# Token group outside, three passes inside: reordering the matmuls of a feature tile

## The chip, the cores and the metric

The kernel runs on one core of one Trainium2 chip. The metric is the device time of one execution in microseconds (us); lower is better.

## What is computed

One layer of a hybrid decoder trunk, for a prompt of 1024 tokens and 8 samples of 8 tokens (1088 tokens in all, model width 1024, fp32 throughout), which share all weights:

```
h = rmsnorm(x, norm_ffn1) * (1 + sc1) + sh1
x = x + 0.5 * g1 * (silu(h @ w1_gate) * (h @ w1_up)) @ w1_down
u = rmsnorm(x, norm_mix) * (1 + sc2) + sh2
p = u @ w_in + b_in       # conv value, conv gate, q, k, v, o, gate_a, gate_b, i, f
A = conv module of the conv columns  (GLU, causal depthwise conv 31, layer norm, silu, @ w_conv_out)
B = mLSTM of q, k, v, i, f in chunks of 128, head norm, sigmoid(o) *, @ w_mlstm_out
x = x + g2 * ((sigmoid(gate_a) * A + sigmoid(gate_b) * B) @ w_out)
h = rmsnorm(x, norm_ffn2) * (1 + sc3) + sh3
x = x + 0.5 * g3 * (silu(h @ w2_gate) * (h @ w2_up)) @ w2_down
y = rmsnorm(x, final_norm)
```

The shifts, scales and gates come from `silu(c) @ w_ada + b_ada`. The new convolution and mLSTM states are outputs too.

## The kernel before

Activations lie with features on the 128 partitions and tokens along the free dimension, as 8 feature tiles (`KT`) of 1092 columns. The tokens are cut in three groups, `GROUPS`, of 364, 364 and 360 columns.

**Weight units.** All large products use weight units of 128 x 1024 values, 220 of them in a fixed order. SyncE loads a unit into `w_raw` (two buffers). GpSimd splits it: `w_hi` is the value rounded to fp32r (line 543), `w_lo` the rest (line 545). It overwrites the halves of a buffer only after TensorE has reported that unit as done (`unit_done`). Activations are split in the same way, `u_hi` and `u_lo` (`hid_hi` and `hid_lo` in the feed-forward blocks, `a_hi` and `a_lo` for the convolution output).

**The three passes.** A product with fp32 quality is the sum of three fp32r products: hi weights with hi activations, hi weights with lo activations, lo weights with hi activations. `three_passes` (line 570) issues them for one feature tile `k`: pass outside, token group inside, nine matmuls. Each group accumulates in a PSUM bank of its own: `slots[:, s, g, ...]`, where a slot `s` of two has three banks.

**Who calls it.** `project` (line 579) handles a unit that is 8 feature tiles of one output tile: 8 x 9 = 72 matmuls. `project_pair` (line 594) does two units at once, alternating between them per tile. `down` (line 611) uses a unit for four output tiles with two feature tiles each, again 72 matmuls. The one unit that runs beside the gate rows (lines 693 to 702) calls it as well; the nine matmuls of line 697, with weights of 36 columns, are written out there and keep their own order.

**What stands around it.** TensorE waits, ahead of the nine matmuls, for the split weights (`w_split`), a free slot (`slot_free`) and where needed for the tile's activations (`ready`). The only increment is on the last matmul of a unit or part. The readers, VectorE and ScalarE, then take all three banks of the slot in one instruction (`bank3`).

**The heads.** The middle of the kernel runs over 4 heads. In `section_a` TensorE does 8 units while VectorE computes the 31 convolution taps of two tiles (`taps`, recorded as line 1072). In `section_b` the units are interleaved with small fp32 matmuls of the mLSTM, the pieces (lines 740 to 775), which write `bank_x` and `bank_y`. Half of a tile's pieces are issued after its nine matmuls (`between`), the other half inside `three_passes` (`middle`), ahead of the third pass. The first piece of a head waits for VectorE's taps and what follows them (line 748 in the waits).

TensorE records one LDWEIGHTS row and one MATMUL row for each fp32r matmul; an fp32 matmul appears as two of each.

Of the kernel before, what the change touches and what calls it, by code (L numbers as in the profile page):

```python
# [37 lines left out]
GROUPS = [(0, GW), (GW, 2 * GW), (2 * GW, NT)]  # L38
# [89 lines left out]
def trunk(nc, t_in, t_out):  # L128
    with ExitStack() as ctx:
# [12 lines left out]
        def own(name, shape, dt=F32):  # L142
            return place(name, shape, dt, region(int(np.prod(shape[1:])) * 4))
# [3 lines left out]
        w_hi = own("w_hi", [P, 2, D], F32R)  # L147
        w_lo = own("w_lo", [P, 2, D], F32R)
# [408 lines left out]
        def _(pe):  # L557
# [10 lines left out]
                return s  # L568

            def three_passes(s, w_of, hi, lo, k, K, middle=None):  # L570
                for q, (w, r) in enumerate(((w_hi, hi), (w_hi, lo), (w_lo, hi))):
                    if middle and q == 2:
                        middle(k)
                    for g, (a, b) in enumerate(GROUPS):
                        last = pe.matmul(slots[:, s, g, 0:b - a], w_of(w), r[:, k, a:b],  # L575
                                         start=(k == 0 and q == 0), stop=(k == K - 1 and q == 2))
                return last

            def project(hi, lo, ready=None, base=0, between=None, middle=None):

                s = open_slot()
                u = jobs.unit.n % 2
                pe.wait_ge(w_split, jobs.unit(1))
                for k in range(KT):
                    if ready is not None:
                        pe.wait_ge(ready, base + k + 1)
                    last = three_passes(s, lambda w: w[:, u, k * P:(k + 1) * P], hi, lo, k, KT, middle)
                    if k == KT - 1:
                        last.then_inc(unit_done, 1)
                    if between:  # L590
                        between(k)
                jobs.take_unit()

            def project_pair(hi, lo, ready, base=0, between=None):

                s, u = open_slot(), jobs.unit.n % 2
                pe.wait_ge(slot_free[1 - s], jobs.used(1))
                pe.wait_ge(w_split, jobs.unit(2))
                for k in range(KT):
                    pe.wait_ge(ready, base + k + 1)  # L600
                    for n in range(2):
                        v = (u + n) % 2
                        last = three_passes((s + n) % 2, lambda w: w[:, v, k * P:(k + 1) * P], hi, lo, k, KT)
                        if k == KT - 1:
                            last.then_inc(unit_done, 1)
                    if between:
                        between(k)
                jobs.take_unit()
                jobs.take_unit()

            def down():

                pe.wait_ge(hid_ready, hid())
                for half in range(2):
                    u = jobs.unit.n % 2
                    pe.wait_ge(w_split, jobs.unit(1))
                    for m in range(4):
                        s = open_slot()
                        for k in range(2):
                            last = three_passes(s, lambda w: w[:, u, k * 512 + m * P:k * 512 + (m + 1) * P],  # L620
                                                hid_hi, hid_lo, k, 2)
                        if m < 3:
                            last.then_inc(part_done, 1)
                            jobs.take_part()
                        else:
                            last.then_inc(unit_done, 1)
                            jobs.take_unit()
# [84 lines left out]
            for n in range(4):  # L712
# [3 lines left out]
                for j in range(4):  # L716
# [3 lines left out]
                    else:  # L720
                        a = NP + (4 * (n - 2) + j) * TB
# [946 lines left out]
```

## Time and profile before

| | us |
|---|---|
| median of 3 runs | 3418.8 |
| lowest and highest | 3417.13, 3423.22 |
| span of the profiled execution | 3417.0 |
| PE busy in it | 3167.0 |
| DVE busy | 1597.9 |
| GpSimd (POOL) busy | 1020.0 |
| ScalarE (ACT) busy | 465.6 |

The times are those of whole executions, the profile is of one of its own. PE is the matmul part of TensorE and PEld its weight loads. Rows of matmuls overlap: what one matmul costs in a stream is the distance from start to start. In a timeline a row merges instructions of a kind, named after the first; its us run from the first start to the last end.

### The profile page before, as it was taken

What the parts mean: (1) busy time and instruction counts of PE and PEld (TensorE: products, weight loads), DVE (VectorE), ACT (ScalarE), POOL (GpSimd) and SP (SyncE); (2) the same over time, 40 slices, a digit from 0 to 9 for tenths busy, and PEclk for the clock granted to TensorE, in tenths of its full rate; (3) what the DMA queues carried; (4) which work ended last, traced back from release to release, by engine and by line L of the source; (5) the groups of instructions that cost most, each with busy time, mean ns of one, the idle gap of its engine ahead of it and who ended that gap; (6) DMA issues with size and microseconds to landing.
All of it is one profiled execution on the core that took longest, in us unless ns stands there. A gap on an engine that the chain in (4) does not pass through costs nothing.

```text
span 3417.0 us, 47244 instructions
## 1 busy us (share of the span) xinstructions
PE 3167.0 (93%) x18860; PEld 3029.7 (89%) x18860; DVE 1597.9 (47%) x2811; ACT 465.6 (14%) x746; POOL 1020.0 (30%) x449
## 2 busy tenths in 40 slices
PE   8999999999968889879888997989998999999995
PEld 8999999999958778878787895789887999999995
DVE  5122233222276943973694397476344233232335
ACT  2000000000031122012112211322012000000001
POOL 1233333333312311321231142034332333333331
PEclk9999999999989999999999998999998999999997
DMA  6312121212121112212211221222210111111111
GB/s 221 106 62 74 61 74 61 74 61 68 49 75 41 44 42 68 70 34 60 74 50 42 68 70 51 60 103 93 108 50 25 44 44 44 47 43 43 43 43 59
DMA packets 83136, 217.63 MB, mean 64 GB/s; under 512 B 28352, under 2 KB 28480, under 8 KB 82496
## 3 DMA queue, kind: packets, MB, share of 16 engines
q1 hardware_dynamic: 83000, 215.86, 19.7%
q8 instruction: 88, 1.44, 0.2%
q14 instruction: 40, 0.33, 0.0%
q10 hardware_dynamic: 8, 0.00, 0.0%
HBM read 184.03 MB, written 31.81 MB: 63 GB/s over the span
## 4 chain that ended last, share of the span: by engine, by line
PE 73%; DVE 16%; issue 5%; DVEq 3%; POOL 1%; DMA 1%; ACT 1%; SPq 0%; ACTq 0%; POOLq 0%
PE slots L575 61%; DVE y L1072 12%; PE bank_x L637 3%; PE bank_x L758 2%; DVEq L1376 2%; PE bank_x L750 1%; PE bank_x L765 1%; PE bank_y L762 1%; PE bank_y L767 1%; DVE work L1100 1%; PE bank_y L637 1%; DMA w_raw<-w_units_dram 1%; PE bank_y L740 1%; PE bank_x L775 0%; PE bank_x L748 0%
## 5 line engine op out<-in xcount | busy, mean ns | idle before, releaser
L543 POOL TENSOR_TENSOR w_hi<-w_raw,one 128x1024 fp32r<-128x1024 f32 x220 | 437.9, 1990 | 2317.9 <-PE slots L575 2247.3
L575 PE MATMUL slots<-u_hi,w_hi 128*128 128x364 f32 (+1 forms) x4032 | 930.3, 339 | 53.0 <-DVE u_lo L1133 20.2
L575 PE MATMUL slots<-u_hi,w_lo 128*128 128x364 f32 (+1 forms) x4032 | 899.5, 332 | 0.0
L575 PE MATMUL slots<-u_lo,w_hi 128*128 128x364 f32 (+1 forms) x4032 | 898.4, 331 | 0.0
L575 PEld LDWEIGHTS slots<-u_hi,w_hi 128*128 128x128 f32 x4032 | 699.4, 191 | 81.4 <-issue 65.4
L575 PEld LDWEIGHTS slots<-u_hi,w_lo 128*128 128x128 f32 x4032 | 705.3, 190 | 9.2 <-issue 8.7
L575 PEld LDWEIGHTS slots<-u_lo,w_hi 128*128 128x128 f32 x4032 | 708.2, 191 | 0.0
L545 POOL TENSOR_TENSOR w_lo<-w_raw,w_hi 128x1024 fp32r<-128x1024 f32 x220 | 581.3, 2642 | 17.2
L1163 DVE TENSOR_TENSOR work<-work,slots 128x1092 f32<-128x1092 f32 x44 | 56.9, 1292 | 913.5 <-PE slots L575 913.5
L1072 DVE SCALAR_TENSOR_TENSOR y<-glu,dw_cur,y 128x1024 f32 (+1 forms) x240 | 344.7, 1436 | 9.1
L1072 DVE SCALAR_TENSOR_TENSOR x<-slots,m_g,x 128x728 f32<-128x728 f32 x368 | 257.8, 742 | 0.0
L575 PE MATMUL slots<-hid_hi,w_hi 128*128 128x364 f32 (+1 forms) x1056 | 237.4, 333 | 11.1 <-DVE hid_lo L1168 9.6
L575 PE MATMUL slots<-hid_lo,w_hi 128*128 128x364 f32 (+1 forms) x1056 | 233.8, 330 | 0.0
L575 PE MATMUL slots<-hid_hi,w_lo 128*128 128x364 f32 (+1 forms) x1056 | 232.3, 328 | 0.0
L575 PEld LDWEIGHTS slots<-hid_hi,w_hi 128*128 128x128 f32 x1056 | 183.6, 190 | 12.1 <-DVE hid_lo L1168 10.0
L885 ACT ACTIVATE hid_hi<-work 128x1092 fp32r<-128x1092 f32 x44 | 49.2, 1118 | 1030.5 <-PE slots L575 733.7
L575 PEld LDWEIGHTS slots<-hid_lo,w_hi 128*128 128x128 f32 x1056 | 183.5, 189 | 0.0
L575 PEld LDWEIGHTS slots<-hid_hi,w_lo 128*128 128x128 f32 x1056 | 183.3, 189 | 0.0
L1146 DVE TENSOR_TENSOR xs_tmp<-slots,m_g 128x64 f32<-128x64 f32 x184 | 41.4, 225 | 289.1 <-PE slots L575 288.1
L1072 DVE SCALAR_TENSOR_TENSOR y<-glus,dw_cur,y 128x64 f32 (+1 forms) x240 | 149.3, 622 | 0.0
L637 PEld LDWEIGHTS bank_x<-cs,ada 128*128 128x128 f32 x896 | 119.4, 212 | 5.3 <-issue 5.3
L637 PE MATMUL bank_x<-cs,ada 128*128 128x9 f32 x896 | 116.2, 267 | 5.3 <-DMA ada<-ada_units_dram 5.3
(219 smaller groups left out, 2187.4 us busy)
## 6 DMA issues: line engine op xcount, KB each, us to landing
w_raw<-w_units_dram SPq DMA_DIRECT2D x220, 512.0 KB, 3.6
ada<-ada_units_dram SPq DMA_DIRECT2D x72, 512.0 KB, 4.2
st<-state_dram SPq DMA_DIRECT2D x32, 257.0 KB, 3.7
C_s_out<-st SPq DMA_DIRECT2D x32, 257.0 KB, 3.6
x_keep<-x SPq DMA_DIRECT2D x1, 4368.0 KB, 12.7
ga_keep<-th SPq DMA_DIRECT2D x8, 546.0 KB, 5.6
gb_keep<-th SPq DMA_DIRECT2D x8, 546.0 KB, 5.6
th<-gb_keep SPq DMA_DIRECT2D x8, 546.0 KB, 4.6
```

The lines of the kernel that those rows point to most:

```text
L543: pool.tensor_tensor(w_hi[:, slot, :], w_raw[:, slot, :], one[:].to_broadcast([P, D]), ALU.mult).then_inc(w_hi_done, 1)
L545: pool.tensor_tensor(w_lo[:, slot, :], w_raw[:, slot, :], w_hi[:, slot, :].bitcast(F32), ALU.subtract).then_inc(w_split, 1)
L575: last = pe.matmul(slots[:, s, g, 0:b - a], w_of(w), r[:, k, a:b], start=(k == 0 and q == 0), stop=(k == K - 1 and q == 2))
L637: last = pe.matmul(b[:, 16 * j:16 * j + NV], ada[:, j, k * P:(k + 1) * P], cs[:, k, :], start=(k == 0), stop=(k == KT - 1))
L740: pe.matmul(bank_y[0:L, 0:L], k_of(m, a, L), q_of(m, a, L), start=(m == 0), stop=(m == 1))
L750: last = pe.matmul(bank_x[0:L, n * P:(n + 1) * P], src, ident[:], start=True, stop=True)
L758: last = pe.matmul(bank_x[0:L, 0:C1], q_of(m, a, L), mem[:, m, :], start=(m == 0), stop=(m == 1))
L885: act.activation(hid_hi[:, j, :], prod, ACT.Copy).then_inc(hid_hi_done, 1)
L1072: return dve.scalar_tensor_tensor(out=out, in0=in0, scalar=scalar, in1=in1, op0=op0, op1=op1)
L1146: dve.tensor_tensor(sample3(xs_tmp[:]), sample3(slots[:, s, 2, LP:LP + NB * TB]), per_batch(g[:, 1:NV]), ALU.mult)
L1163: dve.tensor_tensor(tile3(prod), tile3(sg), bank3(s), ALU.mult).then_inc(slot_free[s], 1)
L1376: dve.drain()
```

## The change

The two loops in `three_passes` change places: the token group becomes the outer loop and the pass the inner one. The call of `middle`, before ahead of the third pass, is now ahead of the third group. The `start` and `stop` flags keep their conditions.

```diff
             def three_passes(s, w_of, hi, lo, k, K, middle=None):
-                for q, (w, r) in enumerate(((w_hi, hi), (w_hi, lo), (w_lo, hi))):
-                    if middle and q == 2:
+                for g, (a, b) in enumerate(GROUPS):
+                    if middle and g == 2:
                         middle(k)
-                    for g, (a, b) in enumerate(GROUPS):
+                    for q, (w, r) in enumerate(((w_hi, hi), (w_hi, lo), (w_lo, hi))):
                         last = pe.matmul(slots[:, s, g, 0:b - a], w_of(w), r[:, k, a:b],
                                          start=(k == 0 and q == 0), stop=(k == K - 1 and q == 2))
                 return last
```

## Rows read from the trace of the kernel before

**Rows 1.** The page: busy time of TensorE, and granted clock in 40 slices.
```profile
PE 3167.0 (93%) x18860; PEld 3029.7 (89%) x18860; DVE 1597.9 (47%) x2811; ACT 465.6 (14%) x746; POOL 1020.0 (30%) x449
...
PEclk9999999999989999999999998999998999999997
```

**Rows 2.** The page: the chain that ended last, share by engine.
```profile
PE 73%; DVE 16%; issue 5%; DVEq 3%; POOL 1%; DMA 1%; ACT 1%; SPq 0%; ACTq 0%; POOLq 0%
```

**Rows 3.** Groups by line: count, busy us, mean ns, idle before.
```profile
L575 PE MATMUL slots<-u_hi,w_hi 128*128 128x364 f32 (+1 forms) x4032 | 930.3, 339 | 53.0 <-DVE u_lo L1133 20.2
L575 PE MATMUL slots<-u_hi,w_lo 128*128 128x364 f32 (+1 forms) x4032 | 899.5, 332 | 0.0
L575 PE MATMUL slots<-u_lo,w_hi 128*128 128x364 f32 (+1 forms) x4032 | 898.4, 331 | 0.0
L575 PEld LDWEIGHTS slots<-u_hi,w_hi 128*128 128x128 f32 x4032 | 699.4, 191 | 81.4 <-issue 65.4
```

**Rows 4.** The chain in order of time: start us, us, what.
```profile
175.23 36.02 PE slots L575 x216
...
2819.89 160.14 PE slots L575 x964
```

**Rows 5.** Timeline of PE from 2999.9 us: start us, us, what.
```profile
2999.97 0.66 PE L575 MATMUL slots<-u_hi,w_hi 128*128 128x364 f32 x3
3000.47 0.67 PE L575 MATMUL slots<-u_lo,w_hi 128*128 128x364 f32 x3
3000.98 0.65 PE L575 MATMUL slots<-u_hi,w_lo 128*128 128x364 f32 x3
3001.47 0.66 PE L575 MATMUL slots<-u_hi,w_hi 128*128 128x364 f32 x3
3001.96 0.66 PE L575 MATMUL slots<-u_lo,w_hi 128*128 128x364 f32 x3
```

**Rows 6.** Busy time by stretch, with the granted clock after the engines.
```profile
150.00:956.00 806.00, 802.02 (x5032) 801.92 (x5031) 227.00 (x393) 47.33 (x43) 270.31 (x122) 1.00 0.19 65
2640.00:3230.00 590.00, 590.00 (x3554) 590.00 (x3553) 171.76 (x288) 36.34 (x33) 218.74 (x98) 1.00 0.14 44
```

**Rows 7.** The waits: us in total, times, longest us.
```profile
DVE work L1163 <- PE slots L575: 913.5, 44, 37.1
```

**Rows 8.** Timeline of the weight loads in the stretch of rows 5.
```profile
3000.31 0.52 PEld L575 LDWEIGHTS slots<-u_lo,w_hi 128*128 128x128 f32 x3
3000.81 0.52 PEld L575 LDWEIGHTS slots<-u_hi,w_lo 128*128 128x128 f32 x3
```

**Rows 9.** Pieces in the timeline; durations min/median/max of lines 758 and 740.
```profile
1253.85 0.59 PE L765 MATMUL bank_x<-vws,ktok 128*128 128x257 f32 x2
1254.28 0.60 PE L767 MATMUL bank_y<-vws,ktok 128*128 128x257 f32 x2
...
1256.30 0.25 PE L740 MATMUL bank_y<-qkvo 128*8 128x8 f32 x4
...
1261.90 1.03 PE L758 MATMUL bank_x<-st,qkvo 128*8 128x257 f32 x4 [0.29 <-DVE b_cur L1072]
...
L758 PE MATMUL bank_x<-st,qkvo x128: 377/380/635, 1220.6 to 2232.6; 128*8 128x257 f32 x128
...
L740 PE MATMUL bank_y<-qkvo x256: 169/224/426, 1178.0 to 2228.3; 128*128 128x128 f32 x64, 128*8 128x8 f32 x64
```

**Rows 10.** The waits of PE: the first piece of a head.
```profile
PE bank_x L748 <- DVE ap_h L1465: 80.9, 4, 25.5
```

**Rows 11.** The chain in order of time: single tiles of nine matmuls.
```profile
1550.90 1.48 PE slots L575 x9
1553.25 1.50 PE slots L575 x9
```

**Rows 12.** Timeline of PE: nine matmuls with 36-column weights, and the next.
```profile
1005.55 0.65 PE L697 MATMUL slots<-u_hi,wg_hi 128*36 128x364 f32 x3
...
1007.00 0.66 PE L575 MATMUL slots<-u_hi,w_hi 128*128 128x364 f32 x3
```

## The prediction

> **What bounds the kernel now.** I read the page's engine lines first: TensorE (PE) is busy 3167.0 of 3417.0 us, and the granted clock stands at 9 in nearly every slice [rows 1]. A busy PE is not yet a bound, so the chain of work that ended last came next: 73% of it is PE and 16% VectorE (DVE) [rows 2]. The groups by line then say which PE work it is: the three kinds of matmul of line 575 come to 4032 each with `u`, and each kind's weight loads are as many as its matmuls [rows 3]. That last point matters here: every matmul loads its own weights, even where the same weights were loaded just before.
>
> Next I looked for the true price of one matmul. The durations in the groups (331 to 339 ns) overlap and are no price; the step from one start to the next is. In the chain, 216 matmuls take 36.02 us and 964 take 160.14 us without a piece of anything else between them [rows 4], so 0.1668 and 0.1661 us each. I take 0.166 us. The timeline of one such stretch shows the same step by step: three matmuls of a pass every 0.49 to 0.51 us [rows 5]. The granted clock there is 1.00, the level of 2.4 GHz [rows 6]. A mean of 362.7 columns (364, 364, 360) at one column a cycle would be 151.1 ns, so 15 ns a matmul are something else. What they are decides the rivals.
>
> **The change part by part.** `three_passes` is called for all 220 weight units. Each has 8 groups of 9 matmuls: 72, in all 15,840, as against 3 x (4032 + 1056 + 192) in the trace. The change permutes the nine inside each group. Nothing is added or removed: the same nine products, the same nine weight loads, the same columns read. Times of one execution: 3417.0 us is the span of the profiled one, 1.8 us under the median of the runs shown, so the sum is made on 3417.0 and 1.8 is added.
>
> Term 1, the waits. Every wait of PE stands ahead of the first of the nine and asks for both halves of the activations, and every increment is on the last of the nine of a unit. DVE reads all three banks of a slot at once and waits for that last one; it waits 913.5 us in total for it at line 1163 [rows 7]. The last matmul stays the ninth, so no reader starts sooner or later. GpSimd, which waits for the same increment, is not moved either. The mLSTM pieces called by `middle` ran after the sixth matmul and still do (before: between pass 2 and pass 3; after: between group 2 and group 3). No DMA is issued from this code and no queue is passed. Cost 0.
>
> Term 2, the weights. The old order changes the stationary data twice per group of nine (to `w_lo`, and back to `w_hi` at the next tile); the new one six times. That is 4 more changes on each feature tile. Whether a load of other data costs more than one of the same data can be read at the old changes. A weight load starts 0.01 us after the preceding matmul started and lies beside it: loads at 3000.31 and 3000.81, matmuls at 3000.47 and 3000.98 that use them [rows 5, 8]. The three-matmul steps that hold a change are 0.51 and 0.49 us, those without are 0.50 and 0.49 [rows 5]. So the cost is 0, with an upper bound of some 5 ns from these rows' resolution. I take 0.
>
> The Trainium skill, page "TensorE: Matmul & The Clock Gate", under the steps of a matmul, gives as the reason for a separate load that one can "load once and matmul repeatedly", and under LDWEIGHTS a price of columns / 1.2 ns, 107 ns for 128. By it an order that keeps `w_hi` for six matmuls should be the better one; if the new changes were exposed at that price, 4 x 1504 tiles x 107 ns would add 640 us (an estimate from that page's figure). The trace does not bear out the premise, since the old order reloads every time [rows 3].
>
> Term 3, the accumulation bank. Old: each matmul writes another PSUM bank than the one before. New: six of nine hand-overs stay in the same bank and the same columns (g0 g0 g0 g1 g1 g1 g2 g2 g2), three change. The trace has no such hand-over for the fp32r matmuls of line 575. The nearest rows are the fp32 matmuls of the pieces, each of which is two instructions onto the same bank. Line 758 has four in a row onto `bank_x`, same columns: 1.03 us from first start to last end, 0.380 us one, so (1.03 - 0.38) / 3 = 0.217 us a step [rows 9]. From line 765 to line 767, one step in the same bank and one to the other bank together take 0.43 us, 0.215 each [rows 9]. These are 257 columns at two cycles each, 0.214 us. So a step in the same bank costs at most 3 ns over its columns. A harder case is line 740: four 8-column matmuls onto the same columns of `bank_y` in 0.25 us, one lasting 0.169, so 0.027 us a step [rows 9]; adding onto a value just written does not stall even at that distance, and here it is 364 columns old. From below: the 15 ns of excess might be the price of changing the bank, and would then go. I take 0, between 0 to +3 ns and -15 ns, because the rows with a change of bank (765 to 767) show no such excess.
>
> Term 4, how much of it shows. For a cost per matmul not all 220 units count. In the first half of each head (8 units, 4 heads) DVE's convolution taps end last, and PE then waits at line 748: 80.9 us in 4 waits, 20 us a head [rows 10]. There 576 matmuls could each be 35 ns slower and nothing is seen, and a faster PE gains nothing. Left are 188 units, 1504 tiles: 9024 same-bank hand-overs and 6016 more changes of weights.
>
> Term 5, the fine pattern. The steps are not equal: tiles in the chain take 1.48 to 1.50 us [rows 11] and threes 0.49 to 0.51 [rows 5], in an order that depends on the position. A new order gives a new pattern, and nothing in the trace ties its mean to the old one more closely than these rows: 0.01 us x 1504 = 15 us either way. With 36-column weights the step is 1.45 us for nine, 0.161 [rows 12], so some of the excess goes with the load beside the matmul, not with the bank.
>
> Sum: 3417.0 + 0 + 0 + 0 + 0 = 3417.0, and with 1.8 the forecast is 3418.8, said as 3419.
>
> **The rivals.**
> R1, slower: adding in the same bank stalls. Place: 9024 hand-overs; price at the bound of 3 ns 27 us, 3446 us. It decides from 0.75 ns a hand-over (6.8 us, 0.2%). For it: no fp32r row excludes it. Against: 0.027 us steps at 8 columns.
> R2, faster: the 15 ns are the change of bank. 9024 x 15 ns = 135 us, 3284 us. For it: all matmuls of line 575 change the bank and all show the excess. Against: the step from 765 to 767 changes it and shows none; the steps with narrow weights change it just as often and are shorter.
> The Trainium skill, same page, section "Back-to-back issue gap", gives warm matmuls columns / 2.4 + 2.5 ns, 154 ns for 364 columns, 12 ns under what the rows show; it does not say in which bank its stream accumulates. By that estimate R2's end would be 9024 x 12 = 108 us faster.
> R3, slower: a change of weights costs the 5 ns that the rows leave open. 6016 x 5 = 30 us, 3449 us. Against: of the two kinds of three that hold a change, one takes 0.51, but the other 0.49, as the shortest without one does [rows 5].
> R4: the pattern of term 5 moves the mean, 3404 to 3434 us. That is the widest way in which the step could move without a cause that I can name.
> That the change does nothing at all is no rival of its own: it can't be told from the forecast but by the order of the rows.
>
> **How the numbers follow.** Forecast 0.75. R1 0.07, R3 0.04, R2 0.05, R4 beyond 0.2% (about what a measurement of this kernel can tell from no change) 0.09, split 0.04 slower and 0.05 faster. So slower 0.15, faster 0.10, same 0.75. The range: from R4's lower end to most of R1, 3405 to 3440; outside are R2, R3 and the last of R1.
>
> **What would show it.** In the profile after, weight loads and matmuls of line 575 must be as many as before; the rows must alternate `u_hi,w_hi`, `u_lo,w_hi`, `u_hi,w_lo` one by one. Term 1 is right if PE's waits keep their totals. Terms 2, 3 and 5 are right if the long pure stretches of the chain keep 0.166 us a matmul; 0.168 would be R1, 0.156 R2. Then the steps inside a bank and at its change tell R1 and R2 apart, and the steps ahead of `w_lo` R3. Term 4 is right if, with a slower step, the 80.9 us at line 748 shrink. The prediction is wrong if the step moves by more than 0.5 ns on average.

## The result

The changed kernel takes 3410.09 us (median of 7 runs, 3406.72 to 3413.51) against 3422.74 us of the kernel before in the same set: ratio 0.9972, 95% interval 0.9961 to 0.9983. It is faster by 0.28% by the ratio, some 10 us; the two medians stand 12.7 us apart, those of a second set 9.3 us, with ratio 0.9976 (0.9965 to 0.9986). The time lies in the range forecast, but I had forecast no change; a gain of over 0.2% had a chance of 0.10.

Of the profile after, first the page: busy time of the engines and the granted clock. Against [rows 1], the clock has the same shape and PE's busy time is 6.8 us less.

```profile
PE 3160.2 (93%) x18860; PEld 3022.9 (89%) x18860; DVE 1597.7 (47%) x2811; ACT 466.0 (14%) x746; POOL 1020.0 (30%) x449
...
PEclk9999999999979989989998998999998999999997
```

The groups by line of the kernel after:

```profile
L575 PE MATMUL slots<-u_hi,w_hi 128*128 128x364 f32 (+1 forms) x4032 | 1371.2, 340 | 53.4 <-DVE u_lo L1133 20.6
L575 PE MATMUL slots<-u_lo,w_hi 128*128 128x364 f32 (+1 forms) x4032 | 1333.7, 331 | 0.0
L575 PE MATMUL slots<-u_hi,w_lo 128*128 128x364 f32 (+1 forms) x4032 | 1329.8, 330 | 0.0
```

The counts are those of [rows 3]. The busy times are half as large again (930.3 to 1371.2), yet nothing got longer: the mean of one is 340 against 339 ns. A group's busy time is the time covered by its rows. Before, three rows of one kind overlapped each other; now each row overlaps only rows of other kinds, so each kind covers more time. Who compares the busy columns of the groups would look for a loss of some 440 us in each of the three groups, which PE's line on the page denies.

That the order is the new one, the timeline of PE shows: the kinds take turns, one row each.

```profile
3001.08 0.33 PE L575 MATMUL slots<-u_hi,w_hi 128*128 128x364 f32 x1
3001.24 0.33 PE L575 MATMUL slots<-u_lo,w_hi 128*128 128x364 f32 x1
3001.42 0.33 PE L575 MATMUL slots<-u_hi,w_lo 128*128 128x364 f32 x1
```

The waits have not moved, but for the one that absorbs. Of the waits after, the rows that answer to [rows 7] and [rows 10]:

```profile
DVE work L1163 <- PE slots L575: 910.2, 44, 37.2
...
PE bank_x L748 <- DVE ap_h L1465: 81.9, 4, 25.9
```

PE's wait at line 748 grew from 80.9 to 81.9 us: a faster PE waits longer there for the convolution taps, and this part of the gain is lost. VectorE's wait for PE is 3.3 us shorter for the same reason.

Where the time went is in the chain. Before, the second feed-forward block had this stretch of 62 units without anything else between (start us, us, what):

```profile
2607.06 744.50 PE slots L575 x4464
```

and after, with the stretch that answers to the first of [rows 4]:

```profile
178.79 35.79 PE slots L575 x216
...
2606.15 739.76 PE slots L575 x4464
```

The same 4464 matmuls take 4.74 us less. Not all of this is the order. The stretch begins behind a wait of 3 us, and soon after it the granted clock is 0.50, the level of 1.2 GHz. Of the kernel before, PE's timeline and the stretch 2608 to 2612 us (PE, PEld, DVE, ACT and POOL, then the granted clock and the DMA's two columns):

```profile
2608.10 1.11 PE L575 MATMUL slots<-u_lo,w_hi 128*128 128x364 f32 x3
2609.01 1.11 PE L575 MATMUL slots<-u_hi,w_lo 128*128 128x364 f32 x3
...
2608.00:2612.00 4.00, 4.00 (x14) 4.00 (x14) 0.06 (x1) 0.00 (x0) 3.92 (x2) 0.50 0.48 135
```

Three matmuls take 0.91 us there, 0.303 each. Of the x4464 stretch, 20 steps of the kernel before are longer than 0.2 us, 2.8 us over the price of the others; after, 13 are, 1.6 us. How many there are differs between executions of one kernel, too: in a second one of the changed kernel 1. The mean of all other steps in the stretch is 166.1 ns before and 165.3 after, so the order is worth 3.5 of the 4.74 us. Over the whole kernel such steps cancel in the comparison: 223 before and 222 after take 0.28 to 0.32 us.

The 216 take 0.23 us less (36.02 before), and a turn of the first block, from one such stretch to the next, 78.56 us (178.79 to 257.35) in place of 78.86 (175.23 to 254.09), some 3 us over its ten turns. The rest is in the other stretches of line 575. From the first to the last matmul of line 575 it is 8.6 us less; the first one came 2.8 us later in this profiled execution (runs of both orders show either start), so the span of 3411.3 us is only 5.7 us shorter. No wait was removed: **each matmul's step at the full clock became shorter**, on average 0.8 ns in that stretch.

### The profile page after: what moved, and what is told of

The parts are those of the page before. It is cut to its first block, busy times and chain, and to the rows that moved or that the text cites. A ratio compares the mean times of both kernels' runs of the same rounds, so it can differ in the third digit from the quotient of the medians.

```text
span 3411.3 us, 47244 instructions
## 1 busy us (share of the span) xinstructions
PE 3160.2 (93%) x18860; PEld 3022.9 (89%) x18860; DVE 1597.7 (47%) x2811; ACT 466.0 (14%) x746; POOL 1020.0 (30%) x449
## 4 chain that ended last, share of the span: by engine, by line
PE 73%; DVE 16%; issue 5%; DVEq 3%; POOL 1%; DMA 1%; ACT 1%; SPq 0%; ACTq 0%; POOLq 0%
PE slots L575 61%; DVE y L1072 12%; PE bank_x L637 3%; PE bank_x L758 2%; DVEq L1376 2%; PE bank_x L750 1%; PE bank_x L765 1%; PE bank_y L762 1%; PE bank_y L767 1%; DVE work L1100 1%; PE bank_y L637 1%; DMA w_raw<-w_units_dram 1%; PE bank_y L740 1%; PE bank_x L775 0%; PE bank_x L748 0%
## 5 line engine op out<-in xcount | busy, mean ns | idle before, releaser
L575 PE MATMUL slots<-u_hi,w_hi 128*128 128x364 f32 (+1 forms) x4032 | 1371.2, 340 | 53.4 <-DVE u_lo L1133 20.6
L575 PE MATMUL slots<-u_lo,w_hi 128*128 128x364 f32 (+1 forms) x4032 | 1333.7, 331 | 0.0
L575 PE MATMUL slots<-u_hi,w_lo 128*128 128x364 f32 (+1 forms) x4032 | 1329.8, 330 | 0.0
L575 PEld LDWEIGHTS slots<-u_hi,w_hi 128*128 128x128 f32 x4032 | 768.5, 191 | 89.6 <-issue 74.1
L575 PEld LDWEIGHTS slots<-u_lo,w_hi 128*128 128x128 f32 x4032 | 770.3, 191 | 1.8
L575 PEld LDWEIGHTS slots<-u_hi,w_lo 128*128 128x128 f32 x4032 | 767.5, 190 | 0.0
L575 PE MATMUL slots<-hid_hi,w_hi 128*128 128x364 f32 (+1 forms) x1056 | 348.7, 330 | 11.2 <-DVE hid_lo L1168 9.6
L575 PE MATMUL slots<-hid_lo,w_hi 128*128 128x364 f32 (+1 forms) x1056 | 348.8, 330 | 0.0
L575 PE MATMUL slots<-hid_hi,w_lo 128*128 128x364 f32 (+1 forms) x1056 | 345.3, 327 | 0.0
L575 PEld LDWEIGHTS slots<-hid_hi,w_lo 128*128 128x128 f32 x1056 | 199.7, 189 | 0.0
## 6 DMA issues: line engine op xcount, KB each, us to landing
x_keep<-x SPq DMA_DIRECT2D x1, 4368.0 KB, 12.7
```

## What a mean hides

The x216 and x4464 rows give means. The start times of the single rows say more. I took the distance from each start to the next between 2830 and 3200 us, and averaged it by its place among the 72 matmuls of a unit (8 tiles of 9). Three tiles of the kernel before, ns (a column is named by the streamed activations and the token group):

```
          hi·g0  hi·g1  hi·g2  lo·g0  lo·g1  lo·g2  hi·g0  hi·g1  hi·g2
tile 2    163.3  165.8  170.9  165.0  167.5  165.8  162.5  164.2  165.8
tile 5    165.0  165.9  166.7  165.8  174.2  166.7  160.8  168.3  159.2
tile 7    165.0  167.5  165.8  162.5  166.7  164.1  182.5  175.9  162.5
```

and of the kernel after:

```
          hi·g0  lo·g0  hi·g0  hi·g1  lo·g1  hi·g1  hi·g2  lo·g2  hi·g2
tile 2    162.5  165.9  162.5  165.9  163.3  166.7  164.1  163.3  166.7
tile 5    165.0  165.8  167.5  160.9  172.5  159.1  165.9  165.0  161.6
tile 7    167.5  165.9  164.1  164.2  164.1  165.0  169.1  163.3  167.5
```

The step is no constant with noise. It is a fixed pattern between 158 and 183 ns, which comes back in every `u` unit of this stretch, in both weight buffers and both slots; the steps at one place differ among themselves by 0.4 to 0.5 ns on average. A unit gains 46 ns; 28 of them are what the 182.5 and the 175.9 in tile 7 of the kernel before lie over the changed kernel's mean. In the forecast I had seen 1.48 and 1.50 us for nine [rows 11] and called it the fine pattern. The mean over the 72 places is 166.0 ns before and 165.4 after; for the `hid` units (`down`) it is 166.4 and 165.2. These means are what the experiments are read by, with the length of the x4464 stretch. Two executions of the changed kernel gave 739.76 and 738.18 us for it, with equal patterns; the first has 13 steps over 0.2 us in it, the second 1. So under 3 us there mean nothing unless the number of such steps is the same.

The pattern also depends on what ran before the unit. In the first feed-forward block small fp32 matmuls run ahead of many units. There the kernel before has the same instructions at the same addresses, but in tiles 1 to 7 of a `u` unit 48 of 62 places differ by over 1 ns from the stretch above, by up to 8 ns, with a mean of 165.7 ns in place of 166.0. In the changed kernel no place differs by more than 0.1 ns. That another engine's accesses make the pattern is unlikely: in the changed kernel's heads, beside VectorE's taps, the medians of the 72 places are those of this stretch to 1 ns.

## The experiments

### Bank or operands

Three reasons were open: the bank (R1 and R2), the weights (R3), and the order in which the streamed columns follow each other (R4). The bank can be cut loose from the order of the operands: let pass q write bank q. With the group outside, the banks then turn with each matmul, as before the change; with the pass outside they stay for three. The first kernel of the set is the changed one again.

> The changed kernel once more, as the control of this set. Every theory expects 9 to 12 us less than the kernel before, and long pure stretches of line 575 at 0.1654 us a matmul against 0.1660 before (means of the starts in the stretch 2830 to 3200 us).

Measured: 3410.3 us, ratio 0.9976 (0.9965 to 0.9986), mean step 165.37 ns.

```diff
                 for g, (a, b) in enumerate(GROUPS):
...
                     for q, (w, r) in enumerate(((w_hi, hi), (w_hi, lo), (w_lo, hi))):
-                        last = pe.matmul(slots[:, s, g, 0:b - a], w_of(w), r[:, k, a:b],
-                                         start=(k == 0 and q == 0), stop=(k == K - 1 and q == 2))
+                        last = pe.matmul(slots[:, s, q, 0:b - a], w_of(w), r[:, k, a:b],
+                                         start=(k == 0 and g == 0), stop=(k == K - 1 and g == 2))
```

> Operand order of the changed kernel (token group outside), but pass q writes bank q, so the banks turn 0 1 2 as in the kernel before; the three groups' sums are mixed in one bank, so what is computed downstream is not the reference's. The reductions over features get one extra 4-column matmul each (7 in all, under 1 us), so that no column stays unwritten. Theory A (the step depends on which operands follow each other, not on the bank): as the changed kernel, 0.1654 us a matmul, about 10 us under before. Theory B (staying in a bank is what saves): 0.1660 us a matmul and no gain, within 3 us of before.

Measured: 3413.26 us, ratio 0.9984 (0.9975 to 0.9993); 165.37 ns. All 72 steps are those of the changed kernel to 0.1 ns. The median lies 3 us over that of the control, and the intervals overlap. In the profiled executions the two differ in the clock: 20 steps over 0.2 us in the x4464 stretch against 1.

```diff
                 for q, (w, r) in enumerate(((w_hi, hi), (w_hi, lo), (w_lo, hi))):
...
                     for g, (a, b) in enumerate(GROUPS):
-                        last = pe.matmul(slots[:, s, g, 0:b - a], w_of(w), r[:, k, a:b],
-                                         start=(k == 0 and q == 0), stop=(k == K - 1 and q == 2))
+                        last = pe.matmul(slots[:, s, q, 0:b - a], w_of(w), r[:, k, a:b],
+                                         start=(k == 0 and g == 0), stop=(k == K - 1 and g == 2))
```

> Operand order of the kernel before (pass outside), but pass q writes bank q, so that three matmuls in a row stay in one bank and the same columns, as in the changed kernel; sums are mixed and downstream values are not the reference's, and the reductions get the same extra 4-column matmul. Theory A (operand order): 0.1660 us a matmul, no gain. Theory B (bank): 0.1654 us a matmul, about 10 us under before.

Measured: 3422.21 us, ratio 1.0007 (0.9998 to 1.0016); 166.00 ns, all steps those of the kernel before to 0.15 ns. The chain's rows, first with banks turning and the group outside:

```profile
179.80 35.79 PE slots L575 x216
...
2609.30 740.94 PE slots L575 x4464
```

then with banks staying and the pass outside:

```profile
178.07 36.02 PE slots L575 x216
...
2613.38 744.42 PE slots L575 x4464
```

Theory A holds and B falls: the step goes with the operands. A change of bank or adding in the same bank costs nothing that 0.1 ns of the mean would show, and both R1 and R2 are out.

The third kernel of the set keeps the banks and changes the order of two passes:

```diff
-                    for q, (w, r) in enumerate(((w_hi, hi), (w_hi, lo), (w_lo, hi))):
+                    for q, (w, r) in enumerate(((w_hi, hi), (w_lo, hi), (w_hi, lo))):
```

> Token group outside, but the passes in the order hi weights with hi activations, lo weights with hi activations, hi weights with lo activations. Same banks as the changed kernel, same number of weight changes, another neighbour for each operand. Theory B (bank): exactly the changed kernel's step, 0.1654 us. Theory A (which operands follow each other): a third value, a few tenths of a ns away on either side of 0.1654, so 3410 us with up to 10 us either way, and another pattern of steps inside a tile.

Measured: 3415.64 us, ratio 0.9991 (0.9982 to 1.0000); 165.75 ns with a pattern of its own; its x4464 stretch is 741.35 us, between the other two. The gain is thus not that of the loop order as such.

### Weights or streamed columns

What of the operands counts, their weights or their streams? Four kernels change one thing each in the changed kernel. First the weights' tensor:

```diff
-                    for q, (w, r) in enumerate(((w_hi, hi), (w_hi, lo), (w_lo, hi))):
+                    for q, (w, r) in enumerate(((w_hi, hi), (w_hi, lo), (w_hi, hi))):
```

> Token group outside, third pass with the hi weights in place of the lo weights: the stationary data change once per feature tile instead of six times; the lo weights' share of the product is left out. Theory W (changing the weights costs something, paid six times in the changed kernel): a step below 0.1654 us. Theory C (the step depends on where in SBUF the streamed columns and the weights loaded beside them lie; lo lies 8192 bytes after hi in every partition, and the pattern in the trace is the same for the two weight buffers, 4096 bytes apart): no difference, 0.1654 us and the same 72 steps to 0.2 ns; time as the changed kernel, 3410 within 4 us.

Measured: 3412.18 us, ratio 0.9977 (0.9967 to 0.9986), 165.37 ns, and the same 72 steps to 0.1 ns. In the chain:

```profile
2606.45 739.76 PE slots L575 x4464
```

To the hundredth of a microsecond the length of the changed kernel's stretch (13 steps over 0.2 us in both), with one change of weights per tile in place of six: a change of weights costs nothing, and R3 is out. Then the place of the weights within the unit:

```diff
-                    last = three_passes(s, lambda w: w[:, u, k * P:(k + 1) * P], hi, lo, k, KT, middle)
+                    last = three_passes(s, lambda w: w[:, u, 0:P], hi, lo, k, KT, middle)
```

(and so in the other calls.)

> The changed kernel with every matmul of a unit taking the first 128 columns of the unit's weights, in place of columns k*128 to (k+1)*128; what is computed is not the reference's. The streamed columns, their order and the banks stay. Theory C with a weight address that matters: another pattern for feature tiles 1 to 7. If only the address within 512 bytes matters: the same pattern to 0.2 ns. Theory D: the same pattern.

Measured: 3409.49 us, ratio 0.9969 (0.9957 to 0.9980), 165.37 ns, x4464 in 739.73 us. 41 of the 72 steps move by over 0.2 ns, up to 0.9 ns, so the expectation of the same pattern to 0.2 ns was not met, but the pattern is recognisably the same and its mean unchanged. Where in the unit the weights lie has a small part in single steps and none in the mean.

The streams are the opposite case. The lo activations replaced by the hi ones:

```diff
-                    for q, (w, r) in enumerate(((w_hi, hi), (w_hi, lo), (w_lo, hi))):
+                    for q, (w, r) in enumerate(((w_hi, hi), (w_hi, hi), (w_lo, hi))):
```

> The changed kernel with the hi activations in the second pass in place of the lo activations; the share of the lo activations is left out. Three matmuls in a row stream the same columns from the same addresses. Theory C: another pattern in all nine positions that follow from the second pass, and another mean, up to 1 ns from 0.1654 us. Theory D: the same 72 steps to 0.2 ns. If re-reading the same columns were cheaper, the mean would fall well below 0.165 us.

Measured: 3421.87 us, ratio 1.0005 (0.9995 to 1.0014), 165.85 ns (`hid` 166.18), another pattern: 66 of the 72 steps differ by over 0.2 ns. Streaming the same columns three times in a row is no cheaper; it lost the gain. And the same order with the activations moved:

```diff
+        region(64)
         u_hi = own("u_hi", [P, KT, W], F32R)
```

> The changed kernel with 64 unused bytes between the weights and the activations in SBUF, so that all activations move by 64 bytes against the weights; instructions, order and computation are the same. Theory C (addresses): another pattern of 72 steps, with a mean that may lie up to 1 ns to either side of 0.1654 us, 3410 us with 15 us either way. Theory D (the pattern comes from the instruction stream, its fetch or dispatch, not from data addresses): the same 72 steps to 0.2 ns.

Measured: 3418.08 us, ratio 0.9996 (0.9986 to 1.0005), 165.76 ns, another pattern. Not an instruction differs from the changed kernel, only 64 bytes of placement (of the activations and all that lies behind them), and most of the gain is gone:

```profile
2610.90 741.47 PE slots L576 x4464
```

Theory D, that the pattern comes from the instruction stream, falls here. What counts is where in SBUF the streamed columns lie, in which order they are visited, and what ran before. That it is the streamed columns' place, and not that of another buffer behind them, rests on `group_out_hi_only` and the next run, which change nothing but PE's streams.

### Does a step have one price per address?

If so, a table of start addresses would predict any order. I tested it in two ways. All matmuls stream from tile 0, column 0:

```diff
-                        last = pe.matmul(slots[:, s, g, 0:b - a], w_of(w), r[:, k, a:b],
+                        last = pe.matmul(slots[:, s, g, 0:b - a], w_of(w), r[:, 0, 0:b - a],
```

> Token group outside; every matmul streams the columns 0 to 364 (360) of feature tile 0 of its tensor, in place of its own; what is computed is not the reference's. If each step is set by the streamed start address and nothing before it: two values only, one for the hi and one for the lo tensor, with the 360-column ones 1.7 ns less. If the state left by the matmuls before plays a part: a pattern that repeats over nine, or keeps wandering over the 72. The mean shows how much of the 15 ns over 151.1 ns hangs on the addresses: near 151 if all, near 165 if none.

Measured: 3422.25 us, ratio 1.0003 (0.9994 to 1.0013), 166.60 ns. From tile 3 on, the nine steps repeat exactly:

```
          hi·364 lo·364 hi·364 hi·364 lo·364 hi·364 hi·360 lo·360 hi·360
tile 3    171.0  166.4  164.3  169.2  166.4  164.3  167.3  167.7  163.3
tile 6    171.0  166.4  164.3  169.2  166.4  164.3  167.3  167.7  163.3
```

The first and the fourth stream the same 364 columns from the same address with the same weights, and the same kind of matmul follows both; they take 171.0 and 169.2 ns. What differs is the bank, which was shown to have no part, and what was streamed before. The third and the sixth stream these columns too and take 164.3; there the weights and both neighbours differ. So the step has a memory, and there is no price per address. Tiles 0 to 2 show it settling into the cycle. Then the streams' starts, all put on a multiple of 64 bytes:

```diff
+            def start_at(k, a, n):
+                up, down = -(k * W + a) % 16, (k * W + a) % 16
+                return a + up if a + up + n <= NT else a - down
...
-                        last = pe.matmul(slots[:, s, g, 0:b - a], w_of(w), r[:, k, a:b],
+                        last = pe.matmul(slots[:, s, g, 0:b - a], w_of(w), r[:, k, start_at(k, a, b - a):start_at(k, a, b - a) + b - a],
```

> Token group outside; each matmul's first streamed column is moved by 0, 4, 8 or 12 columns so that all streams start on a multiple of 64 bytes (without it three of four do not); the number of columns is unchanged, what is computed is not the reference's. Theory C64 (the start within 64 bytes sets the step): the 72 steps fall to two values, 364 and 360 columns, and the mean is the same as in pass_out_aligned to 0.1 ns. Otherwise: still a pattern, and the two orders differ.

> The kernel before (pass outside) with the same moved starts; what is computed is not the reference's. Theory C64: the same two values and the same mean step as group_out_aligned, so the order makes no difference. Otherwise another mean, some tenths of a ns away.

Measured: 3408.71 us, ratio 0.9968 (0.9954 to 0.9981), 165.09 ns with the group outside; 3415.74 us, ratio 0.9986 (0.9977 to 0.9996), 165.55 ns with the pass outside. In `u` units steps from 159 to 173 ns remain, and the two orders still differ by 0.46 ns. Theory C64 falls: the start within 64 bytes is not what sets the step.

### Is the new order better, or only luckier?

The last question decides what to carry away. Both orders, with 32, 64 and 128 unused bytes ahead of the activations; the computation is unchanged in all of them.

> The kernel before (pass outside) with the same 64 unused bytes between weights and activations as in the run group_out_u_shift64; the computation is unchanged. Theory C1 (the mean step is a matter of how this order meets these addresses): a third mean, anywhere from 165.4 to 166.4 ns, so that the gain of 0.6 ns of the new order is not kept at this placement. Theory C2 (group outside is better whatever the addresses, because the streamed columns come in an order that suits): at least 0.4 ns above the 165.76 ns of group_out_u_shift64.

> The kernel before (pass outside) with 32 unused bytes between weights and activations; the computation is unchanged. Theory C1 (order and placement together set the mean): a mean step for u between 165.3 and 166.3 ns that can't be told from the others. Theory C2' (group outside wins on most placements, the 64 bytes being an exception): at least 0.3 ns above group_out_u_shift32.

> The changed kernel (group outside) with the same 32 bytes. C1: between 165.3 and 166.3 ns for u, above or below pass_out_u_shift32, the times of the two within 0.3% of each other. C2': at least 0.3 ns under pass_out_u_shift32, 5 us or more faster.

> The kernel before with 128 unused bytes between weights and activations. If the streamed address counts only within 128 bytes: the pattern of 72 steps and the mean of the kernel before (166.0 ns). If a larger address counts: another pattern. C2': at least 0.3 ns above group_out_u_shift128.

> The changed kernel with the same 128 bytes. If the address counts only within 128 bytes: the pattern and the mean of the changed kernel (165.4 ns), 10 us under before. If a larger address counts: another pattern, mean between 165.3 and 166.3 ns. C2': at least 0.3 ns under pass_out_u_shift128.

Measured, with the two kernels of this case and the run of above in their places (the medians of before in the sets were 3419 to 3421 us):

```
bytes   pass outside: us, ratio, ns of u, hid    group outside: us, ratio, ns of u, hid
  0     3419.6  1        166.0  166.4            3410.3  0.9976   165.4  165.2
 32     3412.8  0.9979   165.7  165.0            3415.7  0.9986   165.6  165.4
 64     3417.8  0.9995   165.5  166.0            3418.1  0.9996   165.8  165.6
128     3411.4  0.9975   165.6  165.5            3420.2  0.9998   166.0  166.7
```

At 128 bytes the sign is turned round. The chain's rows there, pass outside:

```profile
174.96 35.83 PE slots L576 x216
...
2604.49 739.35 PE slots L576 x4464
```

and group outside:

```profile
175.65 36.02 PE slots L576 x216
...
2608.05 745.04 PE slots L576 x4464
```

Of these 5.7 us, 2.7 are steps over 0.2 us (1 and 20 of them) and 3.0 the order; the medians of the whole kernels stand 8.8 us apart. The two orders have exchanged their parts. Theory C1 holds: order and placement together set the mean, which lies between 165.4 and 166.0 ns for `u`. C2 and C2', that the group belongs outside, fall: at 32 and 64 bytes the intervals of the two overlap (0.9969 to 0.9989 and 0.9976 to 0.9995; 0.9986 to 1.0004 and 0.9986 to 1.0005), and at 128 bytes the old order is the faster one, with intervals that don't (0.9964 to 0.9987 and 0.9988 to 1.0008). That only the address within 128 bytes counts falls too, since a shift by 128 gave two new patterns.

### The load beside the stream

Does the weight load that lies beside each stream make the 15 ns over the columns?

```diff
                 for g, (a, b) in enumerate(GROUPS):
+                    M = P if k in (0, K - 1) else 32
...
-                        last = pe.matmul(slots[:, s, g, 0:b - a], w_of(w), r[:, k, a:b],
+                        last = pe.matmul(slots[0:M, s, g, 0:b - a], w_of(w)[:, 0:M], r[:, k, a:b],
```

> The changed kernel, but in feature tiles 1 to 6 of a unit of eight each matmul loads and uses only the first 32 of its 128 weight columns, so these tiles' share of 96 outputs is left out; the streamed columns, their addresses and order stay. If the weight load beside a stream costs in proportion to its width: 15 ns x 32 / 128, about 4 ns, is left over 151.1 in these tiles, 155 ns a matmul. If it has no part: 165.4 ns and the same steps. From the 36-column rows of the kernel before (1.45 us for nine) one would read 161 ns, so a part of it.

Measured: 3400.01 us, ratio 0.9942 (0.9925 to 0.9958). The mean step of `u` units falls from 165.37 to 164.85 ns, not to 155. That is over all eight tiles; over the six with narrow loads it is 0.7 ns less. The load's own row does get shorter, 109 ns in place of 188. In the chain a project unit takes 11.95 us against 12.01 in the changed kernel, and the long stretch 736.64 us against 739.76. Of these 3.1 us, 1.5 are steps over 0.2 us (1 here, 13 there). So the proportional theory falls, and nearly all of the 15 ns are there with 32 columns too. Whether the load costs even the 0.5 ns is not shown: nearly every step is another one than in the changed kernel, by up to 11 ns, and a shift of the addresses moves the mean as far.

The 161 ns that I had expected from [rows 12] were a misreading of one tile. Line 697 has seven tiles of nine at the full clock; their mean steps run from 162 to 168 ns, 165.6 on average, and rows 12 are the shortest. Another of them takes 1.51 us for nine (1012.54 to 1014.05 us).

From the first to the last matmul of the profiled executions this kernel gains 13.2 us over the changed one. About half of it comes from a place that I had not looked at: the first matmul behind a small fp32 one. The changed kernel:

```profile
1260.85 0.43 PE L575 MATMUL slots<-u_hi,w_hi 128*128 128x364 f32 x1
1261.11 0.33 PE L575 MATMUL slots<-u_lo,w_hi 128*128 128x364 f32 x1
```

and with narrow weights:

```profile
1255.18 0.36 PE L576 MATMUL slots<-u_hi,w_hi 128*32 128x364 f32 x1
1255.37 0.33 PE L576 MATMUL slots<-u_lo,w_hi 128*32 128x364 f32 x1
```

The step is 0.26 us and 0.19. At the 197 such places in tiles 1 to 6 its mean is 287 ns in the changed kernel and 248 here, 7.5 us in all; at the 112 others, where the width is the same, it is 285 and 283. The steps under 0.2 us, some 15,000, are 0.4 ns shorter on average, another 6 us. So the load's width costs at most 0.7 ns in the pure stream, and some 40 ns behind a small matmul.

## Why the prediction was wrong

**The bound and the step of 0.166 us** were read rightly: PE bounds the kernel, and the whole gain is in its pure stretches. The price comes out of both of [rows 4] once one knows that their us include the whole of the last matmul, 0.33 us: without it 0.1660 us a step in both. The 0.1668 that I read in the stretch of 216 was this, and not a slower step.

**Term 1, waits: right.** All of PE's waits kept their totals within 1 us.

**Term 2, weights: right at 0.** The run with one change of weights per tile had the same steps to 0.1 ns. The bound of 5 ns was only the resolution of the rows. The price that the Trainium skill gives for a load (page "TensorE: Matmul & The Clock Gate", section "LDWEIGHTS") is not exposed in the pure stream: six changes a tile or one, the time is the same.

**Term 3, bank: right at 0**, shown by the two kernels that cut it loose. R1 and R2 are out, and with them the idea that the 12 ns above the figure of the Trainium skill (page "TensorE: Matmul & The Clock Gate", section "Back-to-back issue gap": columns / 2.4 + 2.5 ns, there for a single isolated matmul) have to do with turning banks. With 7 to 31 ns over the columns from place to place, no fixed addition to the columns describes this stream.

**Term 4, what shows: right in kind.** PE's wait at line 748 took up 1.0 us.

**Term 5 is the step that failed.** Its bound of 15 us either way held the result, but I put its centre at 0 and gave only 0.09 to its going beyond 0.2%. I argued that nothing tied the new mean to the old one more closely than 0.01 us a tile, and then trusted that it was tied. (The 0.161 us for narrow weights, from which I concluded that some of the excess goes with the load, was the shortest of seven tiles.) The runs show the size: a new order moved the mean by -0.6 ns in `u` units and -1.2 ns in `hid` units, and at the four placements the two orders stood -0.28%, +0.07%, 0.0% and +0.23% apart. Two of four go beyond 0.2%. R4 should have had a chance of about a half, equally to either side. Moreover R4 was called a movement without a cause that I can name; the cause can be named as far as this: the order of the streamed addresses, with what was streamed before.

The means could have been read before: the start times of the 72 places, averaged, show steps of 159 to 183 ns that repeat from unit to unit. A pattern that is fixed by the sequence is changed by any new sequence. I had looked at sums of three and nine and took the spread for noise.

What stays open is what in the chip remembers: the runs show that the stream's address and what was streamed before set the step, and that the weights' tensor and the bank do not. The weights' place moves single steps by up to 0.9 ns and not the mean; their width changes the pattern and moves the mean by 0.5 ns. They do not show the unit that does it.

## What to carry to other kernels

When all waits, counts and widths of a dense matmul stream stay, its step can still move by half a percent through the order and the placement of what it streams. Such a gain belongs to the pair of order and address: test the change at two or three placements (some bytes of padding) before it is called an improvement, and test again after the next change to the layout. Average the start-to-start distances by place in the loop body; what looks like jitter in single rows may be a fixed pattern, and two patterns can be compared to 0.1 ns in one execution, where the time of the kernel varies by 0.2%. Leave out the steps at the lower clock, and count them: two executions of the changed kernel have 222 and 196, which alone is 3.5 us.

## What the hardware showed that I had not expected

The fp32r matmuls with 364 columns step at 158 to 183 ns, mean 165.1 to 166.6 from kernel to kernel in `u` units, at a granted clock of 1.00; one cycle a column at 2.4 GHz would be 151.7. At a granted clock of 0.50 the same matmuls step at 303.3 ns on average with 364 columns and 300.0 with 360, which is one cycle a column at 1.2 GHz and nothing over: the 15 ns exist at the higher clock alone. The steps repeat to 0.1 ns from one execution to another, and with all streams from one address they run in a cycle of nine in which equal matmuls take 171.0 and 169.2 ns. Staying in a PSUM bank, turning through three, and changing the weights each cost nothing that 0.1 ns of the mean would show. Loading 32 weight columns in place of 128 comes with a mean step 0.5 ns shorter in the stream, but takes some 40 ns off the first step behind a small fp32 matmul. Moving all activations by 32 to 128 bytes changes a kernel of 3.4 ms by up to 10 us.
